# Norms whose reciprocal rms is applied after the product: X turned unscaled, last products by channel half, first products by channel tile

## The chip, the cores and the metric

The kernel runs on one core of one Trainium2 chip. The metric is the device time of one execution in microseconds (us), the median of several. Engines are named as in the profile: PE is TensorE (matmuls; PEld its weight loads), DVE is VectorE, ACT is ScalarE, POOL is GpSimd, SP is SyncE, which only issues loads here. Each engine works through its own instructions strictly in order; semaphores join the engines.

## The reference

The input X (256 tokens x 1024 channels, fp32) goes through nine stages that each add to it: feed-forward, attention with a state-space model, feed-forward (first layer, with modulation by a condition vector c), feed-forward, a mixer of pooling and long convolution ("mix2"), feed-forward, feed-forward, a latent attention ("mix3"), feed-forward, and a last norm. The change is about the norms ahead of the last six stages, which have a gain but no shift:

```python
def rmsnorm(x, g):
    x32 = x.astype(jnp.float32)
    y = x32 * lax.rsqrt(jnp.mean(x32 * x32, axis=-1, keepdims=True) + RMS_EPS)
    return (y * g.astype(jnp.float32)).astype(x.dtype)

def swiglu_2(h, w_gate, w_up, w_down):
    return (jax.nn.silu(h @ w_gate) * (h @ w_up)) @ w_down

# per layer: x = x + 0.5 * swiglu_2(rmsnorm(x, g), ...)
#            x = x + mixer(rmsnorm(x, g), ...)
#            x = x + 0.5 * swiglu_2(rmsnorm(x, g), ...)
# at the end: rmsnorm(x, final_norm_g)
```

The reciprocal rms r is one number per token, so (r x) W = r (x W): it may be applied to the product. In a feed-forward stage only the gate product must have it before the silu; the factor of the up product can be applied to the stage's result. The three norms of the first layer are followed by h (1 + scale) + shift, and keep their form.

## The kernel before

**Stages.** `STAGES` (line 41) lists nine stages, numbered 0 to 8 here: ffn0, mix1, ffn1, ffn2, mix2, ffn3, ffn4, mix3, ffn5. The norm ahead of stage n is norm n; "boundary n" is the stretch from the last product of stage n-1 to the first product of stage n. Norms 3 to 8 have no shift. Norm 9 is the last norm.

**Weights.** All weights pass as panels of 128 x 1024 fp32 (512 KB) through a ring of six slots (`RING`). SP loads a panel into `raw`; ACT makes its fp32r high part `w_hi` (`split_hi`, L177); DVE makes the rest `w_lo` (`split_lo`, L183). Activations are split in the same way, and each product is three matmuls, high x high, high x low, low x high (`product3`, L199). A feed-forward stage has 66 panels: gate, up and down panels for each of 22 tiles of the hidden dimension. Around each boundary the order of panels on DVE is by hand: at the end of each stage DVE and ACT split the first three panels of the next, the fourth comes behind the norm.

**A feed-forward tile f.** PE: gate product, up product (24 matmuls of 256 columns each, into the two halves of one PSUM bank), then the down product of tile f-1 (`token_product`, 12 matmuls of 512 columns into banks 0 to 3, one bank for each of four quarters: two token halves m by two channel halves). After both products ACT takes the silu of the gate (L378), DVE multiplies it by the up product (L411), ACT makes the high part (L381), DVE the low part (L416). DVE's order is: three `split_lo`, then this `hidden(f)`.

**A boundary without shift.** When a quarter of the last product is complete DVE adds it to X (L486, four instructions, in the order of banks). ACT squares and sums each quarter of X (L255), POOL computes r for each token half (`rstd_pool`, L282 and L283), DVE makes a diagonal matrix `diag` of it (L293), PE turns and scales X in one go as a matmul of X with `diag` (L317, 16 fp32 products of 128 x 128, each in two records), ACT writes the high part times the gain (L275), DVE the low part (L303), and the first product of the next stage starts when its first channel tile is there: all eight channel tiles of the gate panel, then all eight of the up panel. The results of stages 0 to 2 are normed and gated before they are added (L493, L500), and norms 0 to 2 have a shift, with two DVE instructions for a channel tile (L306, L308).

**mix2** starts with a product by tokens (panels M2 to M2+3, result copied by ACT at L1595), then has twelve "parts": a channel product, a copy by ACT with a scale (`centre`, L1573), two taps of a short convolution by DVE (L1631, L1634), with one `split_lo` between. A spectrum product (`multiply`, L1645 to L1648) stands between parts 8 and 9, and 10 and 11, on DVE. **mix3** starts with four channel products and a second norm of the latents (`rms_col`, L1901; POOL's power, L1064).

**The end.** Norm 9's r scales X and the row `final_row` (L2124); the row is loaded by POOL behind its last r (L2051); POOL issues the two halves of the output (L2054).

## Time and profile before

| | us |
|---|---|
| median of 3 runs | 1715.95 (1714.08 to 1716.29) |
| span of the profiled execution | 1713.4 |
| PE busy | 1581.6 |
| DVE busy | 1058.8 |
| ACT busy | 716.8 |
| POOL busy | 263.5 |
| mean granted TensorE clock | 0.959 of full speed |

The span runs from the first to the last instruction; the timed runs lie up to 3 us above it. Matmuls are pipelined: a matmul of 256 columns is shown as 0.28 us, but its successor starts 0.12 us after it; for 512 columns these are 0.39 and 0.23 us. So starts, not durations, tell how long PE takes. The granted clock is given as a share of 2.4 GHz: 0.5 is 1.2 GHz.

### The profile page before, as it was taken

To read this page: it belongs to the slowest core of one execution; us is meant where nothing else is said; L and a number is where in the kernel's file an instruction comes from. 1 tells how busy PE (TensorE), PEld (TensorE's weight loads), DVE (VectorE), ACT (ScalarE), POOL (GpSimd) and SP (SyncE) were. 2 spreads that over 40 slices of the span, in tenths; PEclk is the share of its full clock that TensorE was granted. 3 is DMA by queue.
4 is the path that set the end of the run, shared out by engine and by line. 5 is a ranking of instruction groups with operands and counts; after the bars stand their busy time and mean duration, and the time that the engine had idled before them with its cause. 6 is when DMAs were issued, how large, how long until landed. Compare 5 with 4: busy or idle time off the path is not lost.

```text
span 1713.4 us, 28025 instructions
## 1 busy us (share of the span) xinstructions
PE 1581.6 (92%) x10288; PEld 1417.2 (83%) x10288; DVE 1058.8 (62%) x1344; ACT 716.8 (42%) x1145; POOL 263.5 (15%) x264
## 2 busy tenths in 40 slices
PE   4899869899789999899999999999999988999996
PEld 1599858775569999899988789998999987889995
DVE  7779994699566555555555755555555548655553
ACT  3344322432344444544444444444544436454442
POOL 1489951144310000100000000000000000000000
PEclk9799978898989999999999999999999999999998
DMA  6599755340036665655554335555555532245551
GB/s 219 217 335 335 256 190 197 128 135 25 25 111 216 217 217 183 239 184 184 184 160 148 111 124 183 186 186 174 172 184 184 184 123 99 74 148 184 184 184 50
DMA packets 80195, 292.79 MB, mean 171 GB/s; under 512 B 9019, under 2 KB 9372, under 8 KB 79564
## 3 DMA queue, kind: packets, MB, share of 16 engines
q1 hardware_dynamic: 74432, 270.71, 46.7%
q0 software_dynamic: 4784, 19.09, 3.1%
q10 hardware_dynamic: 924, 2.25, 0.4%
q8 instruction: 36, 0.59, 0.1%
q14 instruction: 19, 0.16, 0.0%
HBM read 288.87 MB, written 3.15 MB: 170 GB/s over the span
## 4 chain that ended last, share of the span: by engine, by line
PE 66%; DVE 3%; ACT 3%; POOL 1%; issue 1%; DMA 0%; DVEq 0%; ACTq 0%; POOLq 0%
PE bank L199 61%; PE bank L317 1%; PE bank L1488 1%; ACT arena L255 1%; DVE w_lo L183 1%; PE bank L1501 1%; ACT w_hi L177 0%; PE bank L1812 0%; PE bank L1790 0%; PE bank L1801 0%; ACT h_hi L275 0%; ACT arena L1884 0%; DVE arena L493 0%; POOL arena L1285 0%; ACT arena L1869 0%
## 5 line engine op out<-in xcount | busy, mean ns | idle before, releaser
L199 PE MATMUL bank<-h_hi,w_hi 128*128 128x256 f32 x2376 | 683.8, 288 | 20.7 <-DVE h_lo L308 7.1
L199 PE MATMUL bank<-h_lo,w_hi 128*128 128x256 f32 x2376 | 677.1, 285 | 0.0
L199 PE MATMUL bank<-h_hi,w_lo 128*128 128x256 f32 x2376 | 676.7, 285 | 0.0
L183 DVE TENSOR_TENSOR w_lo<-raw,w_hi 128x1024 fp32r<-128x1024 f32 x458 | 562.1, 1276 | 98.1 <-ACT w_hi L177 96.8
L199 PEld LDWEIGHTS bank<-h_hi,w_hi 128*128 128x128 f32 x2376 | 460.6, 194 | 35.0 <-DVE h_lo L308 9.3
L177 ACT ACTIVATE w_hi<-raw 128x1024 fp32r<-128x1024 f32 x458 | 453.8, 1049 | 31.9 <-PE bank L199 30.8
L199 PEld LDWEIGHTS bank<-h_lo,w_hi 128*128 128x128 f32 x2376 | 460.9, 194 | 5.7 <-issue 1.0
L199 PEld LDWEIGHTS bank<-h_hi,w_lo 128*128 128x128 f32 x2376 | 460.4, 194 | 0.0
L378 ACT ACTIVATE arena<-bank 128x256 f32<-128x256 f32 x132 | 50.5, 383 | 541.9 <-PE bank L199 541.9
L411 DVE TENSOR_TENSOR arena<-arena,bank 128x256 f32<-128x256 f32 x132 | 55.6, 421 | 343.1 <-ACT arena L378 343.1
L199 PE MATMUL bank<-w_hi,f_hi 128*128 128x512 f32 x528 | 209.2, 396 | 15.2 <-DVE f_lo L416 15.2
L199 PE MATMUL bank<-w_hi,f_lo 128*128 128x512 f32 x528 | 208.8, 396 | 0.0
L199 PE MATMUL bank<-w_lo,f_hi 128*128 128x512 f32 x528 | 207.3, 393 | 0.0
L282 POOL TENSOR_SCALAR stat<-stat 128x1 f32<-128x1 f32 x26 | 9.1, 351 | 1062.7 <-ACT arena L255 1062.3
L199 PEld LDWEIGHTS bank<-w_hi,f_hi 128*128 128x128 f32 x528 | 100.7, 191 | 33.3 <-issue 15.6
L199 PEld LDWEIGHTS bank<-w_lo,f_hi 128*128 128x128 f32 x528 | 100.3, 190 | 22.0
L199 PEld LDWEIGHTS bank<-w_hi,f_lo 128*128 128x128 f32 x528 | 100.8, 191 | 16.2
L381 ACT ACTIVATE f_hi<-arena 128x256 fp32r<-128x256 f32 x132 | 55.2, 418 | 118.7 <-DVE arena L411 118.7
L521 DVE SCALAR_TENSOR_TENSOR arena<-arena,stat 128x1024 f32<-128x1024 f32 x70 | 103.7, 1482 | 1.2
L416 DVE TENSOR_TENSOR f_lo<-arena,f_hi 128x256 fp32r<-128x256 f32 x132 | 64.1, 486 | 52.3 <-ACT f_hi L381 52.3
L317 PE MATMUL bank<-diag,X 128*128 128x128 f32 x288 | 42.4, 317 | 24.8 <-DVE diag L293 24.8
L317 PEld LDWEIGHTS bank<-diag,X 128*128 128x128 f32 x288 | 40.7, 229 | 28.3 <-DVE diag L293 28.3
(285 smaller groups left out, 1315.1 us busy)
## 6 DMA issues: line engine op xcount, KB each, us to landing
raw<-panels SPq DMA_DIRECT2D x458, 512.0 KB, 4.5
arena<-ada SPq DMA_DIRECT2D x56, 512.0 KB, 4.9
arena<-ada POOLq DMA_DIRECT2D x16, 512.0 KB, 3.9
spectrum<-arena POOLq DMA_DIRECT2D x2, 1024.0 KB, 7.2
arena<-rows POOLq DMA_DIRECT2D x4, 512.0 KB, 4.1
arena<-spectrum POOLq DMA_DIRECT2D x1, 2048.0 KB, 13.9
X<-x_in SPq DMA_DIRECT2D x1, 1024.0 KB, 5.3
arena<-decay ACTq DMA_DIRECT2D x2, 512.0 KB, 6.6
```

What stands on the lines that cost most here:

```text
L177: act.activation(w_hi[:, slot, :], raw[:, slot, :], ACT.Copy).then_inc(hi_ready, 1)
L183: dve.tensor_tensor(w_lo[:, slot, :], raw[:, slot, :], w_hi[:, slot, :].bitcast(F32), ALU.subtract).then_inc(lo_ready, 1)
L199: last = pe.matmul(out_ap, a, b, start=start and n == 0, stop=stop and n == 2)
L255: return act.activation(squares[:, q, :], source, ACT.Square, scale=D ** -0.5, accum_out=stat[:, at + q:at + q + 1])
L317: mm = pe.matmul(bank[4 + k // 2][:, at:at + P], X[:, m, k * P:(k + 1) * P], diag[:, m, :], start=True, stop=True)
L378: act.activation(ffn_buf[:, f % 2, :], up_bank(f)[:, 0:SEQ], ACT.Silu).then_inc(silu_done, 1)
L381: act.activation(f_hi[:, f % 2, :], ffn_buf[:, 2 + f % 2, :], ACT.Copy).then_inc(f_hi_done, 1)
L411: dve.tensor_tensor(ffn_buf[:, 2 + f % 2, :], ffn_buf[:, f % 2, :], up_bank(f)[:, SEQ:2 * SEQ], ALU.mult).then_inc(hidden_done, 1)
L416: dve.tensor_tensor(f_lo[:, f % 2, :], ffn_buf[:, 2 + f % 2, :], f_hi[:, f % 2, :].bitcast(F32), ALU.subtract).then_inc(f_lo_done, 1)
L521: dve.scalar_tensor_tensor(out=dst, in0=src, scalar=c, in1=dst, op0=ALU.mult, op1=ALU.add).then_inc(ada_used, 1)
L1488: mm = pe.matmul(bank[first_bank + 2 * f + s][:, :], forward[:, s, m, f * P:(f + 1) * P], z_tok[:, m, :], start=m == 0, stop=m == MT - 1)
L1501: mm = pe.matmul(bank[BACK_BANKS[c]][:, 0:SEQ], product[:, 2 * f + s, c * P:(c + 1) * P], inverse[:, s, f, :], start=f + s == 0, stop=f + ...
```

## The change

- **Norms 3 to 8.** X is transposed as it stands, each channel tile when its quarters of X are added, with no wait for r. The turned banks are laid out by channel half. r comes later: ACT squares two quarters ahead of the copies of the high parts and two behind them; POOL and DVE make `diag` behind the eighth low part; behind the first product PE multiplies a matrix of ones with `diag` (`row_pe`), ACT copies the result to `rstd_row` (r along the free axis, the same in all partitions).
- **Where r is applied.** In a feed-forward stage DVE multiplies each gate product by `rstd_row` into `gate_buf`, ACT takes the silu from there, and the result is added to X with r/2. The DVE waits for the gate panel alone, then for the silu, then for the up panel. The up product has a bank of its own. In mix2 ACT's copy of the first product has the scale r, and DVE multiplies each of the twelve parts by `rstd_row` (`scale_part`) ahead of the split of the next panel. In mix3 the latents' mean squares are multiplied by r squared and their diagonals by r, and one more multiplication goes into the keys' rotation.
- **The last two products** of stages 3 to 8 are done by quarters: three quarters of the last but one, two of the last, the fourth of the last but one, the third of the last; the last quarter comes behind the first eight transposes. In front of norms 4 to 8 the order of quarters is channel half 0 of both token halves, then channel half 1.
- **The first product** of every stage is done by channel tile: for a feed-forward stage gate and up of tile k in turn; for mix3 two latent products. This holds for norms 0 to 2 too (mix1 has one panel there).
- **The load** of the last norm's row goes from behind r of norm 9 to behind r of norm 8.

The diff, cut to its core:

```diff
+        def last_two_products(pe, g0, x0, x1, ready, order):
+
+            a, b, c, d = order
+            pe.wait_ge(lo_ready, g0 + 1)
+            for q in (a, b, c):
+                token_quarter(pe, g0, q, *x0, False, False)
+            pe.wait_ge(*ready)
+            pe.wait_ge(lo_ready, g0 + 2)
+            for q in (a, b):
+                token_quarter(pe, g0 + 1, q, *x1, False, True).then_inc(result_ready, 1)
+            token_quarter(pe, g0, d, *x0, False, False).then_inc(panel_used, 1)
+            token_quarter(pe, g0 + 1, c, *x1, False, True).then_inc(result_ready, 1)
+
+        def last_quarter(pe, at):
+
+            kind, n = STAGES[at]
+            x = (f_hi[:, 1, :], f_lo[:, 1, :]) if kind == "ffn" else (h_hi[:, 7, :], h_lo[:, 7, :])
+            token_quarter(pe, FIRST[(kind, n)] + SIZE[kind] - 1, by_quarter(at)[3], *x, False,
+                          True).then_inc(panel_used, 1)
...
+        PLAIN = 3
+
+        def plain(n):
+
+            return PLAIN <= n < len(STAGES)
+
+        def by_quarter(at):
+
+            return (0, 2, 1, 3) if plain(at + 1) and at >= PLAIN else (0, 1, 2, 3)
...
+        def turned_out(n, k):
+
+            b, half = (4 + k % 4, k // 4) if plain(n) else (4 + k // 2, k % 2)
+            return bank[b][:, half * SEQ:(half + 1) * SEQ]
+
+        def of_channel(n, k):
+
+            return KT * n + (k if plain(n) else k | 1) + 1
...
+        def norm_act(act, n):
+
+            if plain(n):
+                norm_act_squares(act, n, 0, 2)
+                norm_act_rest(act, n)
+                norm_act_squares(act, n, 2, 4)
+            else:
+                norm_act_squares(act, n)
+                if n < len(STAGES):
+                    norm_act_rest(act, n)
+
+        def row_act(act, n):
+
+            act.wait_ge(row_product, rows_before(n) + 1)
+            act.activation(rstd_row[:, :], row_bank(n)[:, 0:SEQ], ACT.Copy).then_inc(row_done, 1)
+
+        def row_bank(n):
+
+            return bank[3 if STAGES[n][0] == "ffn" else 6]
+
+        def row_pe(pe, n):
+
+            pe.wait_ge(diag_done, 2 * n + 2)
+            for m in range(MT):
+                mm = pe.matmul(row_bank(n)[:, m * P:(m + 1) * P], ones[:, :], diag[:, m, :], start=True,
+                               stop=True)
+            mm.then_inc(row_product, 1)
...
+        def turn_pe(pe, n, k, m):
+
+            tr = pe.transpose(turned_out(n, k)[:, m * P:(m + 1) * P], X[:, m, k * P:(k + 1) * P], ident[:, :])
+            if m == MT - 1:
+                tr.then_inc(turned, 1)
+
+        def norm_pe(pe, n, first):
+
+            if plain(n):
+                for m in range(MT):
+                    pe.wait_ge(x_done, added(n, 0, m))
+                    for k in range(4):
+                        turn_pe(pe, n, k, m)
+                if n - 1 >= PLAIN:
+                    last_quarter(pe, n - 1)
+                for k in range(4):
+                    pe.wait_ge(h_lo_done, KT * n + k + 1)
+                    first(k)
+                    for m in range(MT):
+                        pe.wait_ge(x_done, added(n, 1, m))
+                        turn_pe(pe, n, 4 + k, m)
+                for k in range(4, KT):
+                    pe.wait_ge(h_lo_done, KT * n + k + 1)
+                    first(k)
+                row_pe(pe, n)
+                return
...
+            def first_up(k):
+
+                if k == 0:
+                    pe.wait_ge(lo_ready, base + 2)
+                    if s0:
+                        pe.wait_ge(hidden_done, s0)
+                w = slice(k * P, (k + 1) * P)
+                for g, out in ((base, gate_out(at, 0)), (base + 1, up_out(at, 0))):
+                    mm = product3(pe, out, w_hi[:, g % RING, w], w_lo[:, g % RING, w], h_hi[:, k, :],
+                                  h_lo[:, k, :], k == 0, k == KT - 1)
+                    if k == KT - 1:
+                        mm.then_inc(panel_used, 1)
...
+                if plain(at):
+                    act.wait_ge(gate_scaled, gates_before(n) + f + 1 + 2 * i)
+                    act.activation(ffn_buf[:, f % 2, :], gate_buf[:, f % 2, :],
+                                   ACT.Silu).then_inc(silu_done, 1)
+                else:
+                    act.wait_ge(panel_used, base + (3 * f + 1 if f else 2) + RING * i)
+                    act.activation(ffn_buf[:, f % 2, :], gate_out(at, f), ACT.Silu).then_inc(silu_done, 1)
...
+                if plain(at):
+                    if f == 0:
+                        dve.wait_ge(row_done, rows_before(at) + 1)
+                    dve.wait_ge(panel_used, base + (3 * f if f else 2) + RING * i)
+                    if s0 + f >= 2:
+                        dve.wait_ge(silu_done, s0 + f - 1 + 2 * i)
+                    dve.tensor_tensor(gate_buf[:, f % 2, :], gate_out(at, f), rstd_row[:, :],
+                                      ALU.mult).then_inc(gate_scaled, 1)
                 dve.wait_ge(silu_done, s0 + f + 1 + 2 * i)
                 if s0 + f >= 2:
                     dve.wait_ge(f_lo_done, s0 + f - 1 + 2 * i)
-                dve.tensor_tensor(ffn_buf[:, 2 + f % 2, :], ffn_buf[:, f % 2, :],
-                                  up_bank(f)[:, SEQ:2 * SEQ], ALU.mult).then_inc(hidden_done, 1)
+                dve.wait_ge(panel_used, base + (3 * f + 1 if f else 2) + RING * i)
+                dve.tensor_tensor(ffn_buf[:, 2 + f % 2, :], ffn_buf[:, f % 2, :], up_out(at, f),
+                                  ALU.mult).then_inc(hidden_done, 1)
...
+        def add_plain_dve(dve, kind, n, at, i):
+
+            q = by_quarter(at)[i]
+            m, x = q // 2, X[:, q // 2, quarter(q)]
+            wait_result(dve, at, kind, n, q)
+            dve.scalar_tensor_tensor(out=x, in0=bank[q][:, :],
+                                     scalar=stat[:, HALF_RS + m:HALF_RS + m + 1] if kind == "ffn" else 1.0,
+                                     in1=x, op0=ALU.mult, op1=ALU.add).then_inc(x_done, 1)
+
+        def boundary_dve(dve, kind, n, at, order):
+
+            if at < PLAIN:
+                add_dve(dve, kind, n, at)
+                if not plain(at + 1):
+                    diag_dve(dve, at + 1)
+                low_dve(dve, at + 1, order)
+                if plain(at + 1):
+                    diag_dve(dve, at + 1)
+                    half_dve(dve, order)
+                return
+            for i in range(3):
+                add_plain_dve(dve, kind, n, at, i)
+            if plain(at + 1):
+                low_dve(dve, at + 1, order, 0, 1)
+                add_plain_dve(dve, kind, n, at, 3)
+                low_dve(dve, at + 1, order, 1, KT)
+                diag_dve(dve, at + 1)
+                half_dve(dve, order)
+            else:
+                add_plain_dve(dve, kind, n, at, 3)
...
+            def first_tokens(k):
+
+                g, w = M2 + k // 2, slice(512 * (k % 2), 512 * (k % 2) + 512)
                 pe.wait_ge(lo_ready, g + 1)
-                for half in range(2):
-                    k, w = 2 * j + half, slice(512 * half, 512 * half + 512)
-                    pe.wait_ge(h_lo_done, KT * 4 + k + 1)
-                    for m in range(MT):
-                        t = slice(m * P, (m + 1) * P)
-                        mm = product3(pe, bank[m][:, :], w_hi[:, g % RING, w], w_lo[:, g % RING, w],
-                                      h_hi[:, k, t], h_lo[:, k, t], k == 0, k == KT - 1,
-                                      weights_move=True)
-                mm.then_inc(panel_used, 1)
+                for m in range(MT):
+                    t = slice(m * P, (m + 1) * P)
+                    mm = product3(pe, bank[m][:, :], w_hi[:, g % RING, w], w_lo[:, g % RING, w],
+                                  h_hi[:, k, t], h_lo[:, k, t], k == 0, k == KT - 1, weights_move=True)
+                if k % 2:
+                    mm.then_inc(panel_used, 1)
+
+            norm_pe(pe, 4, first_tokens)
...
+            row_act(act, 4)
             act.wait_ge(panel_used, M2 + 4)
             for m in range(MT):
-                act.activation(a_tok[:, m, :], bank[m][:, :], ACT.Copy).then_inc(a_evac, 1)
+                act.wait_ge(rstd_done, 2 * 4 + m + 1)
+                act.activation(a_tok[:, m, :], bank[m][:, :], ACT.Copy,
+                               scale=stat[:, RS + m:RS + m + 1]).then_inc(a_evac, 1)
...
+            def scale_part(j):
+
+                dve.wait_ge(panel_used, M2 + 5 + j)
+                dve.tensor_tensor(part[:, j % 2, :], bank[4 + j % 2][:, 0:SEQ], rstd_row[:, :],
+                                  ALU.mult).then_inc(part_scaled, 1)
+
             def taps_of(j):
 
                 dve.wait_ge(conv_centre, j + 1)
                 tile = (j + 8) % 12
-                src, dst = bank[4 + j % 2], conv[:, j, :]
+                src, dst = part[:, j % 2, :], conv[:, j, :]
...
             dve_panels(dve, M2 + 3, 4)
+            dve.wait_ge(row_done, rows_before(4) + 1)
             for j in range(8):
+                scale_part(j)
                 split_lo(dve, M2 + 7 + j)
                 taps_of(j)
             dve.wait_ge(m2_loaded, 16 * 5)
             for f in range(2):
                 multiply(0, 0, f)
                 for j in (8 + 2 * f, 9 + 2 * f):
+                    scale_part(j)
...
+            order(dve.tensor_tensor(rstd_squared, stat[:, RS:RS + 2], stat[:, RS:RS + 2], ALU.mult))
             dve.wait_ge(latent_sums, 1)
             for j, width in ((0, 256), (2, 128)):
-                dve.tensor_scalar(rms_col[:, j:j + 2], bank[3][:, j:j + 2], 1.0 / width, EPS, ALU.mult,
+                order(dve.tensor_tensor(rms_col[:, j:j + 2], bank[3][:, j:j + 2], rstd_squared, ALU.mult))
+                dve.tensor_scalar(rms_col[:, j:j + 2], rms_col[:, j:j + 2], 1.0 / width, EPS, ALU.mult,
                                   ALU.add).then_inc(rms_mean, 1)
-            diagonals_dve(dve, 4, (rms_pow, 2), latent_diag)
+            dve.wait_ge(rms_pow, 2)
+            for j in range(4):
+                dve.tensor_scalar(rms_diag[:, j, :], ident[:, :], rms_col[:, j:j + 1],
+                                  stat[:, RS + j % 2:RS + j % 2 + 1], ALU.mult,
+                                  ALU.mult).then_inc(latent_diag, 1)
...
+            order(dve.tensor_tensor(k_turn[r, 0, :], k_turn[r, 0, :], k_turn[r, 1, :], ALU.add))
+            dve.wait_ge(row_done, rows_before(7) + 1)
+            dve.tensor_tensor(k_turn[r, 0, :], k_turn[r, 0, :], rstd_row[r, :],
+                              ALU.mult).then_inc(k_rope_done, 1)
...
-                if at + 1 == len(stages):
+                if at == 7:
                     pool.dma_start(final_row, rows[6:7, :].partition_broadcast(P)).then_inc(final_loaded, 16)
```

## Rows read from the trace of the kernel before

**Rows 1.** The page: busy time, share of the span and instructions of PE.
```profile
PE 1581.6 (92%) x10288; PEld 1417.2 (83%) x10288; DVE 1058.8 (62%) x1344; ACT 716.8 (42%) x1145; POOL 263.5 (15%) x264
```
**Rows 2.** Waits of PE: line, releaser, total us, times, longest.
```profile
PE bank L317 <- DVE diag L293: 24.8, 9, 5.4
```
**Rows 3.** Timeline, PE, boundary 6: start us, us, instructions [idle before, releaser].
```profile
1190.36 0.40 PE L199 MATMUL bank<-w_hi,f_hi 128*128 128x512 f32 x1
...
1195.60 0.39 PE L199 MATMUL bank<-w_lo,f_hi 128*128 128x512 f32 x1
1197.54 3.84 PE L317 MATMUL bank<-diag,X 128*128 128x128 f32 x32 [1.55 <-DVE diag L293]
1201.58 0.35 PE L199 MATMUL bank<-h_hi,w_hi 128*128 128x256 f32 x1 [0.20 <-DVE h_lo L303]
```
**Rows 4.** The same timeline, DVE.
```profile
1192.83 1.22 DVE L183 TENSOR_TENSOR w_lo<-raw,w_hi 128x1024 fp32r<-128x1024 f32 x1 [0.53 <-ACT w_hi L177]
1193.99 2.73 DVE L486 SCALAR_TENSOR_TENSOR X<-bank,X 128x512 f32<-128x512 f32 x4
...
1198.55 0.29 DVE L293 TENSOR_SCALAR diag<-ident,stat 128x128 f32<-128x128 f32 x1 [1.07 <-POOL stat L283]
1200.94 3.23 DVE L303 SCALAR_TENSOR_TENSOR h_lo<-bank,C,h_hi 128x256 fp32r<-128x256 f32 x8 [2.11 <-ACT h_hi L275]
```
**Rows 5.** The same timeline, ACT.
```profile
1190.56 0.38 ACT L378 ACTIVATE arena<-bank 128x256 f32<-128x256 f32 x1 [4.37 <-PE bank L199]
...
1196.75 0.63 ACT L255 ACTIVATE arena<-X 128x512 f32<-128x512 f32 x1
...
1200.07 3.03 ACT L275 ACTIVATE h_hi<-bank,C 128x256 fp32r<-128x256 f32 x8 [2.60 <-PE bank L317]
...
1207.77 0.38 ACT L378 ACTIVATE arena<-bank 128x256 f32<-128x256 f32 x1 [2.78 <-PE bank L199]
```
**Rows 6.** Timeline, PE, in mix2: eight plain transposes of 128 x 128.
```profile
928.94 1.03 PE L1511 MATMUL bank<-ident,arena 128*128 128x128 f32 x8
```
**Rows 7.** Busy us (instructions) of PE, PEld, DVE, ACT, POOL by stretch; PEclk, DMA, GB/s.
```profile
200.00:240.00 40.00, 23.17 (x122) 20.67 (x123) 39.96 (x17) 7.33 (x11) 37.86 (x15) 0.72 0.45 157
...
700.00:702.00 2.00, 2.00 (x12) 2.00 (x11) 0.00 (x0) 0.00 (x0) 2.00 (x4) 0.50 0.70 178
...
1190.36:1201.58 11.22, 9.47 (x59) 8.01 (x57) 5.94 (x11) 6.02 (x16) 1.71 (x4) 1.00 0.27 99
...
1480.00:1482.00 2.00, 1.90 (x11) 1.79 (x10) 1.69 (x4) 1.41 (x4) 0.00 (x0) 0.63 0.00 0
```
**Rows 8.** Timeline, DVE, mix2 from the first spectrum product to the last tap.
```profile
943.57 1.23 DVE L183 TENSOR_TENSOR w_lo<-raw,w_hi 128x1024 fp32r<-128x1024 f32 x1
...
960.28 0.48 DVE L1634 SCALAR_TENSOR_TENSOR arena<-bank,C,arena 128x255 f32<-128x255 f32 x1
```
**Rows 9.** Timeline, boundary 3, DVE and PE.
```profile
694.43 2.74 DVE L500 SCALAR_TENSOR_TENSOR X<-arena,stat,X 128x512 f32<-128x512 f32 x4
...
698.35 5.69 PE L317 MATMUL bank<-diag,X 128*128 128x128 f32 x32 [5.41 <-DVE diag L293]
```
**Rows 10.** Timeline, boundary 2: ACT's first silu, and DVE's last low part.
```profile
510.04 0.38 ACT L378 ACTIVATE arena<-bank 128x256 f32<-128x256 f32 x1 [5.12 <-PE bank L199]
...
506.02 0.42 DVE L308 TENSOR_TENSOR h_lo<-arena,h_hi 128x256 fp32r<-128x256 f32 x1
```
**Rows 11.** Timeline, DVE, ffn0: behind its first product, and in its middle.
```profile
89.35 0.42 DVE L411 TENSOR_TENSOR arena<-arena,bank 128x256 f32<-128x256 f32 x1 [3.65 <-ACT arena L378]
...
215.37 14.66 DVE L183 TENSOR_TENSOR w_lo<-raw,w_hi 128x1024 fp32r<-128x1024 f32 x3
```
**Rows 12.** The page's groups: busy us, mean ns | idle of the engine before.
```profile
L411 DVE TENSOR_TENSOR arena<-arena,bank 128x256 f32<-128x256 f32 x132 | 55.6, 421 | 343.1 <-ACT arena L378 343.1
```
**Rows 13.** Timeline, the end: r of norm 9, and the last scaling.
```profile
1699.66 0.56 POOL L283 TENSOR_TENSOR stat<-stat 128x1 f32<-128x1 f32 x1
...
1704.04 2.48 DVE L2124 SCALAR_TENSOR_TENSOR arena<-X,stat,arena 128x1024 f32<-128x1024 f32 x2 [5.61 <-DMA arena<-rows]
```

212 lines of the change are left out of this document (126 added, 86 removed).

## The prediction

> **What bounds the kernel now.** The page first: PE is busy for 1581.6 of 1713.4 us [rows 1], so in most places only less PE work could help, and the change removes nearly none. The waits of PE come next: 24.8 us in 9 pieces, one for each norm, for the diagonal matrix of r [rows 2]. So I read the boundaries. In boundary 6 PE starts the last but one product at 1190.36, issues the last matmul of stage 5 at 1195.60, idles 1.55 us, turns X for 3.84 us and starts stage 6 at 1201.58 [rows 3]. The wait is a relay: DVE adds four quarters from 1193.99 [rows 4], ACT's last square starts at 1196.75 [rows 5], POOL then makes r, DVE the diagonal at 1198.55 [rows 4]; ACT's first high part waits for the turned X until 1200.07 [rows 5], DVE's low part until 1200.94 [rows 4]. Boundaries 4, 5, 7 and 8 repeat this to 0.1 us. Inside a feed-forward tile DVE waits 343.1/132 = 2.6 us for the silu [rows 12]: there PE is the bound, with room on DVE. Last, the end: the final scaling waits 5.61 us, and what ends the wait is a load [rows 13].
>
> **Boundary 6, worked out.** Time t runs from 1190.36, the start of the last but one product. A silu starts 0.20 us after the matmul behind its product (1190.56 against 1190.36), so the second up/gate pair of stage 6 starts at 1207.77 - 0.20, t = 17.2 [rows 3, 5]. This is what the change must bring forward. A quarter of a product is 3 matmuls of (1195.60 - 1190.36)/23 = 0.228 us, so 0.68; a tile of the first pair is 6 matmuls of 0.12, so 0.72 us.
> - The new order has the quarters of the first channel half out at 2.73 and 3.41, the third at 4.78 (each shows 0.2 later). DVE is held by one `w_lo` before its adds. That ends now at t = 3.7 [rows 4]; as the multiplication no longer stands behind the silu (0.4), at 3.3. Adds at 0.68 (a quarter of 2.73 [rows 4]): 3.3 to 4.7, the third 5.0 to 5.7.
> - A plain transpose takes (1.03 - 0.27)/7 = 0.11 us [rows 6], a product with the diagonal 3.84/16 = 0.24 [rows 3]. The first eight: 4.8 to 5.65; then the last quarter to 6.3. ACT's two squares end at 5.4, its first high part (0.49) at 5.95, the low part at 6.5. So the first product starts at 6.5 instead of 11.2: 4.7 us won.
> - Given back: eight more transposes (0.9) and the fourth add, out at 7.2, for which PE waits some 0.4. The eight tiles end at about 13.6. Then the row of r: squares 3 and 4 stand on ACT behind the eighth high part (about 11.1), end at 12.5; POOL takes twice 0.95 (the 0.56 of its power [rows 13] and an addition before it, with gaps), the second r out at 14.0, DVE 0.3: 14.4 with its handovers. PE waits 0.8 for it, issues 0.5, and goes on at 14.9. Here the wait for r comes back, shortened, behind the first product.
> - Sum: 17.2 - 14.9 = **2.3 us**. Lower bound 1.0 (each handover 0.1 worse), upper 3.7 (no wait for the row).
> Behind it DVE splits two panels by 17.0, and PE needs the first at 17.8, the second at 20.7; the first hidden tile is ready by 19.4 and needed at 20.7. The cover is thin but there.
> Boundaries 5, 6 and 8: 3 x 2.3 = **6.9**. Boundary 7 too, but mix3's chain of the latents' rms gets two small ordered instructions (0.2 each, as nothing hides them): **1.9**.
>
> **Boundary 4 and mix2.** The first product of mix2 has 12 matmuls of 512 columns for two tiles, 1.37 us a tile. Tiles 6 and 7 need the fourth panel's `w_lo`, which DVE does behind `diag`, and ACT's `w_hi` behind squares 3 and 4. With a tile each 1.37 us (plus transposes) the eighth high part ends only at 13.4, the squares at 14.8, `diag` at 16.5, `w_lo` at 17.9; PE wanted it at 15.5. So 2.4 us of waiting; the product and its row end at 21.4 instead of 22.2: 0.8 won. Then DVE's stretch from 943.57 to 960.28 + 0.48 = 960.76 [rows 8], where it works nearly through and PE waits for it at both ends: four more multiplications, 4 x 0.42, as an instruction of this size takes [rows 12], and the split at 943.57, which now stands behind the scaling of part 8 and so behind PE. Worked through, the last tap ends 0.8 us later on an unchanged start: 1.6 us lost on the shifted one. Together **-0.8** (-2.5 to +1). The other eight multiplications fall in 2.9 us periods of which 2.7 are then filled: hidden.
>
> **Boundary 3.** The gated adds stay. Now `diag` waits for all of them [rows 9]; then the turned quarters follow the adds of 694.43 to 697.17 directly, ACT copies at 697.0 (two squares first), the first product starts at 698.1 instead of 704.24 (698.35 + 5.69 + 0.20). PE's clock matters here: it idled for 5.41 us and its 16 products took 5.69 us instead of 3.84 [rows 3, 9], at 1.2 GHz until after 702 [rows 7]. I let the slow stretch last until 701.8 also after the change, which costs 1.85 us of the first product. Row of r by 707.0, next pair at 707.5 instead of 710.2: **2.7** (1.5 to 4.6, the latter at full clock).
>
> **Boundaries 2 and 0.** Two DVE instructions a tile pace the first product, and the up product then stands behind. With both products by tile the up product fits: DVE ends at 506.44 [rows 10], PE 0.75 later, at 507.2, instead of 509.84 (510.04 - 0.20): **2.6** (1.5 to 2.9). In ffn0 the same brings 2.6 to 4.5 at first, since PE's clock was low there, and DVE idled 3.65 us behind it [rows 11]. But in the middle of ffn0 DVE is the bound: from 200 to 240 us it is busy 39.96, with POOL at 37.86, PE at 23.17 [rows 7], and three splits take 14.66 us instead of 3.5 [rows 11]. POOL's work doesn't move. What DVE did ahead survives in my reading: **2.5** (0 to 4.5). Boundary 1 has one panel by tile, as before: 0.
>
> **Tiles of ffn2 to ffn5.** 88 multiplications of 0.42 us, and a wait for the silu inside DVE's sequence. Per tile DVE then needs 3.5 for splits, 0.5 waiting for `w_hi`, 0.42 scaling, 0.46 for the silu, 1.32 from the multiplication to the low part: 6.2 of the 8.5 us that PE takes (24 x 2 x 0.12 + 12 x 0.228). PE's row product and the transposes are in the sums above. Cost at nothing; the cover is 2.3 us a tile.
>
> **The end.** Without the load the first scaling can follow the last add, and the second one the second r, out at 1699.66 + 0.56 = 1700.22; with 1.28 us for it (the two take 2.48) it ends at 1701.5 instead of 1706.52 [rows 13]. **5.0** (4.5 to 5.6). The load moves to the start of ffn5 on POOL's queue, where POOL has nothing else; panels there are six ahead.
>
> **Sum.** 6.9 + 1.9 - 0.8 + 2.7 + 2.6 + 2.5 + 5.0 = 20.8 us on the profiled span of 1713.4: 1692.6. The median lies 2.55 above that span: 1715.95 - 20.8 = **1695**. The forecast's own range: 1687 to 1703.
>
> **Rivals.**
> - *The clock falls at the boundaries.* Around 1480, in a stretch of waits and plain transposes, the granted clock was 0.63 [rows 7]; in boundary 6, with idle time and the diagonal products, it stayed at 1.00 [rows 7]. The new boundary has transposes in place of such products. If each of the five boundaries 4 to 8 loses to it what boundary 3 lost (5.69 - 3.84 = 1.85 us [rows 3, 9]), 9.2 is given back: 1704. Against it: the quiet stretch is now 0.9 us of transposes with no idle, less than half the one near 1480. The Trainium skill, "TensorE: Matmul & The Clock Gate", Part 4 on the PE-mode transpose, says that transposes don't count as busy for the clock as matmuls do; the rows near 1480 agree with it, but had idle time too. By that rule boundary 3, too, would keep its slow stretch. Chance 12%.
> - *The relay doesn't shorten.* PE's in-order queue has waits for single adds and single low parts; if a handover I took as done in time is late (the third add, the low part behind it), the first product starts early and stops again, and the row of r ends where the diagonal did. Then boundaries 3 to 8 bring nothing, and 0 and 2 and the end bring 10.1: 1706. Against it: the bare transposes need no r. Chance 8%.
> - *Slower: DVE becomes the bound of the tiles.* Place: hidden(f) of ffn2 to ffn5. The gain of 20.8 and a loss over 3.4 need 24.2/88 = 0.28 us a tile, so a DVE sequence of 8.8 us against my 6.2, 2.6 more than worked out; it decides from 8.5 on. At 8.8 the time is about 1719. For it: DVE now waits three times inside a tile, before only twice; against: its idle time of 2.6 us a tile [rows 12] is more than the 0.9 added. Chance 4%.
> - *The change brings more*: full clock in boundary 3, all of 4.5 kept in ffn0, no wait for the row: 1686. Chance 8%.
>
> **How the numbers follow.** Forecast 68% at 1695; clock 12% at 1704, no relay 8% at 1706, more 8% at 1686, slower 4% at 1719. The range 1686 to 1706 holds all but the slower case and tails. 0.2% is 3.4 us, about what a measurement of this kernel can tell from no change: faster than 1712.5 has 93%, within 1712.5 to 1719.4 3%, slower 4%.
>
> **What would show it.** In boundary 6: no diagonal product; first product of the stage 6.5 us after the last but one product of the stage before begins; a wait of PE of about 0.8 us for `diag` behind the eighth tile. In boundary 4: a wait of some 2.4 us for `w_lo`. In mix2: DVE's last tap later against the first spectrum product. In ffn2 to ffn5: 8.5 us from silu to silu, unchanged. At the end: no wait for a load. Granted clock 1.00 over boundaries 4 to 8. Wrong if silus stand further apart than 8.5 us, if the clock shows 0.5 behind the transposes, or if ffn0 ends no earlier.

## The result, and the profile after

| | before | after |
|---|---|---|
| median | 1715.93 us | 1692.85 us (1686.63 to 1694.82, four runs) |
| ratio after/before | | 0.9867, interval 0.9847 to 0.9887 |
| span of the profiled execution | 1713.4 us | 1692.1 us |
| PE busy | 1581.6 us | 1572.3 us |
| PE waits for `diag` | 24.8 us in 9 | 11.7 us in 3, and 3.5 us in 5 for the row |

Predicted were 1695 us for the median and 1692.6 for the span. The page and the waits of PE, after (what waited, on what, total us, times, longest):

```profile
PE 1572.3 (93%) x10216; PEld 1405.0 (83%) x10216; DVE 1102.4 (65%) x1454; ACT 728.2 (43%) x1151; POOL 263.5 (16%) x264
...
PE bank L424 <- DVE diag L368: 11.7, 3, 5.4
...
PE bank L199 <- DVE w_lo L183: 9.0, 3, 4.5
...
PE bank L356 <- DVE diag L368: 3.5, 5, 0.8
```

The 24.8 us of [rows 2] are now 11.7 (norms 0 to 2, which still have the diagonal product, L424) and 3.5 (the row of r, L356). Boundary 6 in PE's timeline after, and two rows each of ACT and DVE; it answers to [rows 3 to 5]:

```profile
1179.78 0.40 PE L199 MATMUL bank<-w_hi,f_hi 128*128 128x512 f32 x1
...
1184.57 1.03 PE L397 MATMUL bank<-ident,X 128*128 128x128 f32 x8
...
1186.36 0.39 PE L199 MATMUL bank<-h_hi,w_hi 128*128 128x256 f32 x1
...
1190.22 0.38 PE L397 MATMUL bank<-ident,X 128*128 128x128 f32 x2
...
1194.27 0.71 PE L356 MATMUL bank<-diag,ones 128*128 128x128 f32 x4 [0.79 <-DVE diag L368]
...
1191.62 0.62 ACT L294 ACTIVATE arena<-X 128x512 f32<-128x512 f32 x1
...
1193.93 0.28 DVE L368 TENSOR_SCALAR diag<-ident,stat 128x128 f32<-128x128 f32 x1 [0.84 <-POOL stat L330]
```

With t counted from 1179.78 the first eight transposes start at 4.79 (worked out: 4.8), the first product at 6.58 (6.5), the last square at 11.84, the second diagonal at 14.15, the row product at 14.49 after a wait of 0.79 (0.8). PE goes on at 14.96 (14.9); the next pair started at 17.2 before. The end, after ([rows 13]): the second scaling starts 0.04 us after the second r is out (1683.65 + 0.56), and no load stands ahead of it.

```profile
1682.13 1.27 DVE L2357 SCALAR_TENSOR_TENSOR arena<-X,stat,arena 128x1024 f32<-128x1024 f32 x1
...
1683.65 0.56 POOL L330 TENSOR_TENSOR stat<-stat 128x1 f32<-128x1 f32 x1
...
1684.25 1.28 DVE L2357 SCALAR_TENSOR_TENSOR arena<-X,stat,arena 128x1024 f32<-128x1024 f32 x1 [0.84 <-POOL stat L330]
```

To see where the time went, one takes the same instruction in both traces (a silu, an add, the first product behind a stage's second pair) and follows the difference of its two times. What a stretch adds to this difference is what it won in this one execution:

| stretch | predicted | measured |
|---|---|---|
| up to norm 0 | 0 | 0.4 |
| boundary 0 and the rest of ffn0, boundary 1, mix1 | 2.5 | 4.4 + 1.3 - 1.1 = 4.6 |
| boundary 2 | 2.6 | 2.5 |
| boundary 3 | 2.7 | 3.0 |
| boundary 4 and mix2 | +0.8 - 1.6 = -0.8 | -0.9 - 1.3 = -2.2 |
| boundaries 5, 6, 8 | 3 x 2.3 = 6.9 | 3 x 2.2 = 6.6 |
| boundary 7 and mix3 | 1.9 | 1.3 |
| tiles of ffn2 to ffn5 | 0 | 0.0 |
| end | 5.0 | 5.0 |
| sum | 20.8 | 21.3 |

The measured rows are rounded, so they add up to 21.2. Two of them vary between executions by more than they miss by: what lies ahead of ffn1, and boundary 7 with mix3 (first and last experiment).

### The profile page after: what moved, and what is told of

The parts are those of the page before. It is cut to its first block, busy times and chain, and to the rows that moved or that the text cites. A ratio compares the mean times of both kernels' runs of the same rounds, so it can differ in the third digit from the quotient of the medians.

```text
span 1692.1 us, 28192 instructions
## 1 busy us (share of the span) xinstructions
PE 1572.3 (93%) x10216; PEld 1405.0 (83%) x10216; DVE 1102.4 (65%) x1454; ACT 728.2 (43%) x1151; POOL 263.5 (16%) x264
## 4 chain that ended last, share of the span: by engine, by line
PE 67%; DVE 3%; ACT 2%; POOL 1%; issue 1%; ACTq 0%; DVEq 0%; POOLq 0%
PE bank L199 62%; PE bank L1686 1%; PE bank L1699 1%; PE bank L2015 1%; ACT arena L294 1%; PE bank L397 1%; PE bank L2037 1%; DVE w_lo L183 0%; PE bank L2026 0%; POOL stat L330 0%; DVE arena L646 0%; POOL stat L329 0%; ACT arena L2112 0%; POOL arena L1481 0%; ACT arena L2097 0%
## 5 line engine op out<-in xcount | busy, mean ns | idle before, releaser
L524 ACT ACTIVATE arena<-arena 128x256 f32<-128x256 f32 x88 | 36.8, 418 | 195.2 <-DVE arena L565 195.2
L706 DVE SCALAR_TENSOR_TENSOR arena<-arena,stat 128x1024 f32<-128x1024 f32 x70 | 107.9, 1541 | 1.2
L528 ACT ACTIVATE arena<-bank 128x256 f32<-128x256 f32 x44 | 16.8, 382 | 167.0 <-PE bank L199 167.0
L1481 POOL TENSOR_TENSOR arena<-arena 128x512 f32<-128x512 f32 x32 | 46.4, 1471 | 53.6 <-DVE arena L1514 53.6
```

Source lines behind the costliest of these rows:

```text
L524: act.activation(ffn_buf[:, f % 2, :], gate_buf[:, f % 2, :], ACT.Silu).then_inc(silu_done, 1)
L706: dve.scalar_tensor_tensor(out=dst, in0=src, scalar=c, in1=dst, op0=ALU.mult, op1=ALU.add).then_inc(ada_used, 1)
L1481: pool.tensor_tensor(rot_out[:, s % 2, 2 * part:2 * part + 2, :], z, r, ALU.mult).then_inc(rot_done, 1)
```

## The experiments

Executions of one kernel lie up to 11 us apart, so an effect of a few us is read from the traces, stretch by stretch, and the medians only say that nothing contradicts. Where a stretch from norm to norm is given, it runs from one "first eight transposes" row to the next; after has them at 880.18, 993.81, 1184.57, 1375.37 and 1489.84 (norms 4 to 8), so 113.63, 190.76, 190.80 and 114.47 us.

**The changed kernel again**, unedited, on the chip of the next three.

> The changed kernel once more, as the base for the other runs of this chip. All theories expect about 1693 us, a ratio of 0.987 to the kernel before; its single runs so far lay between 1686.6 and 1694.8. In boundary 6 a wait of PE of 0.8 us for the diagonal, in boundary 4 one of 2.4 us for the fourth panel, with the granted clock at 0.5 behind it.

Measured: 1691.16 us, ratio 0.986 (0.9843 to 0.9876). Norm 4 to 5 takes 113.62 us and 5 to 6 takes 190.74: this part repeats to 0.02. What differs between executions lies elsewhere. Up to norm 2 all eleven traces of the changed kernel and of its variants below run the same instructions, yet norm 2's diagonal product starts between 483.46 and 492.64 us in them (488.51 in after, 485.98 in after_again, 493.61 before). Counted as in the table's second row, from norm 0 to norm 2, the win is 4.7 us in after, 7.0 in after_again, and 3.6 to 9.4 in all. Mix3 is the other such place (last experiment).

**The load alone.** The kernel before, with

```diff
-                if at + 1 == len(stages):
+                if at == 7:
                     pool.dma_start(final_row
```

> The kernel before with the load of the last norm's row alone moved behind r of norm 8. The forecast's term is 5.0 us: 1715.9 - 5.0 = 1710.9, ratio 0.9971, and the last scaling ends about 1.3 us behind the second r. Rival: the load at the start of the last stage delays panels there; then the last stage is longer than before and the gain under 4 us.

Measured: 1709.24 us, 5.5 under before's 1714.70 on this chip, ratio 0.9965 (0.9953 to 0.9977). In its trace the second scaling waits for r and no longer for a DMA:

```profile
1699.56 1.40 POOL L283 TENSOR_TENSOR stat<-stat 128x1 f32<-128x1 f32 x1
...
1700.99 1.28 DVE L2124 SCALAR_TENSOR_TENSOR arena<-X,stat,arena 128x1024 f32<-128x1024 f32 x1 [0.45 <-POOL stat L283]
```

The profiled execution is 4.5 us shorter (1708.9 against 1713.4); POOL's last instruction for r took 1.40 us there instead of the 0.56 of before and after, which is not explained. So the term stands by itself at 4.5 to 5.5, a fifth to a fourth of the gain, for one moved line. The last stage is no longer than before: its first down product starts at 1521.96 us against 1522.07, the additions to X at 1695.59 against 1695.69.

**The first pair by channel tile, alone.** The kernel before, in ffn0 and ffn1 with

```diff
-            up(0)
+            if n < 2:
+                ...
+                for k in range(KT):
+                    ...
+                    for g, out in ((base, bank[0][:, 0:SEQ]), (base + 1, bank[2][:, 0:SEQ])):
+                        mm = product3(pe, out, ..., k == 0, k == KT - 1)
+            else:
+                up(0)
```

> The kernel before with the first pair of products of ffn0 and ffn1 done by channel tile (gate and up in turn, the up product in a bank of its own), nothing else. Theory: boundary 2 gains 2.5 us, boundary 0 some 4.4 us, as PE stays busy enough there for a granted clock of 1.00; together 5.5 to 7, time 1709 to 1710.5. Rival, the sum of the prediction: 2.6 + 2.5 = 5.1 with part of the gain of boundary 0 lost where DVE and POOL bound ffn0. Second rival: the clock there differs between executions whatever the order is, and only 2.6 + 2.6 comes.

Measured: 1707.91 us, ratio 0.9959 (0.9947 to 0.9971), 6.8 us less; the sum had 2.6 + 2.5 = 5.1, which the interval (5.0 to 9.1 us) just allows, so the traces must tell. The first silu of ffn0 starts at 83.59 instead of 88.94, and 0.9 of these 5.35 us were won ahead of the first channel tile, so the pair's order brought 4.4. Boundary 2 brought 2.5: the lead over before grows from 7.86 at norm 2's diagonal product (485.75) to 10.38 at the first down product (505.22). First the kernel with only the load moved (its ffn0 is that of before), at 80 to 82 and 84 to 88 us, then this one, then after, at 84 to 88 (columns: PE, PEld, DVE, ACT, POOL busy with counts, granted clock, DMA share, GB/s):

```profile
80.00:82.00 2.00, 1.70 (x7) 1.21 (x8) 1.93 (x5) 1.98 (x2) 0.00 (x0) 0.75 0.00 0
...
84.00:88.00 4.00, 4.00 (x21) 4.00 (x21) 1.83 (x2) 0.00 (x0) 3.94 (x2) 0.52 0.52 145
```
```profile
84.00:88.00 4.00, 4.00 (x36) 4.00 (x35) 2.99 (x5) 2.84 (x4) 3.65 (x4) 1.00 0.72 227
```
```profile
84.00:88.00 4.00, 4.00 (x36) 4.00 (x35) 2.99 (x5) 2.76 (x5) 3.65 (x3) 1.00 0.55 162
```

With one product PE did three matmuls for each channel tile of DVE; the tiles came 0.92 us apart and PE waited 0.30 us for each, and the clock fell near 81 us, inside this product; the up product behind it then ran slowly (84 to 88 us: 0.52). It did so in both traces with one product. With two products interleaved the clock stayed at 1.00 from 80 us to the first silu in all twelve traces, and the order brought 4.4 us in each of them. The pace alone is not the cause, though: in boundary 2 of the same two traces the same single product, with the same waits, ran at 1.00 throughout, and there the order brings 2.5. What makes the difference between the two boundaries was not tested. The 1.9 us between 4.4 and 2.5 is what my 2.5 left at the upper end of its range. They are not lost in the middle of ffn0 either, where DVE and POOL are full: by the end of ffn0 the lead was never smaller than at the first silu (0.6 to 2.4 us larger in the twelve traces).

**Ordinary products in place of transposes.** The changed kernel, X turned by

```diff
-            tr = pe.transpose(..., X[:, m, k * P:(k + 1) * P], ident[:, :])
+            tr = pe.matmul(..., X[:, m, k * P:(k + 1) * P], ident[:, :], start=True, stop=True)
```

> The changed kernel with X turned by an ordinary fp32 product with the identity instead of PE's transpose: 0.24 us instead of 0.10 for each of 16. Theory: the first product of a stage starts 8 x 0.14 = 1.1 us later, each of its first four tiles takes 0.28 more, all of this on the path (the wait for the row of r follows the eighth tile and stays): 2.2 us for each of boundaries 4 to 8 and less for boundary 3, 11 to 12 us in all, about 1704. Rival (the clock): if transposes let the clock fall, ordinary products would hold it up, and the loss would be smaller, in boundary 4 above all.

Measured: 1701.01 us (1694.46 to 1705.13), ratio 0.9906 (0.9886 to 0.9927), 9.9 more than the changed kernel on this chip. The profiled execution had lost 4.1 us to after's before norm 3, where the two kernels are the same; from norm 3 to ffn5 it loses 7.2, less than the 9.9 of the medians and the 11 to 12 expected (1.6 in boundary 6, for 2.2 expected). So the plain transpose is worth a third of the gain by the trace: the first eight take 1.95 us in 16 passes,

```profile
1191.21 1.95 PE L397 MATMUL bank<-ident,X 128*128 128x128 f32 x16
...
1202.51 0.71 PE L356 MATMUL bank<-diag,ones 128*128 128x128 f32 x4 [0.81 <-DVE diag L368]
```

and the row product comes 11.30 us after them instead of 9.70. In boundary 3 it is the other way round. Granted clock there (third to last column), first of after, whose first transposes start at 687.66, then of this kernel, where they start at 691.79:

```profile
690.00:692.00 2.00, 1.60 (x7) 0.61 0.03 8
692.00:694.00 2.00, 2.00 (x12) 0.54 0.00 0
694.00:696.00 2.00, 2.00 (x19) 1.00 0.00 0
```
```profile
692.00:694.00 2.00, 1.83 (x15) 1.00 0.00 0
694.00:696.00 2.00, 1.58 (x14) 1.00 0.05 8
696.00:698.00 2.00, 2.00 (x20) 1.00 0.00 0
```

Both waited 2.29 us for the gated adds. Behind the wait come transposes, or products with the same operands; from four to six us after the first transposes the granted clock was 0.50 in nine traces of ten and 0.57 in the tenth (in one of the nine, extra_8, it had fallen before they began); with products, in the one trace there is, it never left 1.00. The row of r came at 10.96 us behind the first turn instead of 11.43, though PE had twice the passes. The Trainium skill, "TensorE: Matmul & The Clock Gate", Part 4, says that transposes don't count as busy for the clock in the way matmuls do; boundary 3 agrees with it, on one trace with products. One trace is not enough to show it: behind the wait in boundary 4 the clock stayed up in one execution of eight with no change there, and in this very kernel it fell there, from the third matmul behind the wait of 2.37 us on, though X was turned by products.

**The fourth panel earlier.** The changed kernel; DVE and ACT split mix2's fourth panel between channel tiles 4 and 5 of norm 4:

```diff
             for k in range(KT):
+                if n == 4 and k == 4:
+                    split_hi(act, M2 + 3)
                 act.wait_ge(turned, of_channel(n, k))
...
-            act_panels(act, M2 + 3, 4)
+            act_panels(act, M2 + 4, 3)
```

and the same for DVE with `split_lo` and `dve_panels`.

> The changed kernel with mix2's fourth panel split between the fourth and the fifth channel tile of norm 4, on ACT and DVE, instead of behind the diagonal. Theory: PE's wait of 2.36 us in boundary 4 goes, and with it the fall of the granted clock behind it (six matmuls of 512 columns at 0.43 instead of 0.23 us, and the row's product): mix2 starts its parts 4.0 us earlier, -4.0 us in the time, granted clock 1.00 through the boundary. Rival: the clock falls there for another reason (the transposes); then the wait alone goes, -2.4 us, and some window behind the turn still shows less than 1.00.

Measured: 1690.52 us, ratio 0.9866 (0.9845 to 0.9886); median against median only 0.6 less than the changed kernel, which ran on another chip, and by the ratios (0.9866 against 0.986) nothing. In the trace norm 4 to norm 5 takes 109.39 us instead of 113.63: 4.24 less, where 4.0 were expected. What the medians don't show of it lies in the spread of other stretches: this execution came into norm 4 1.15 us later than the one of after, and its five runs lie between 1686.67 and 1695.05. Here is the spot, PE after:

```profile
891.03 0.39 PE L199 MATMUL bank<-w_lo,h_hi 128*128 128x512 f32 x1
893.78 0.47 PE L199 MATMUL bank<-w_hi,h_hi 128*128 128x512 f32 x1 [2.36 <-DVE w_lo L183]
...
895.24 0.63 PE L199 MATMUL bank<-w_hi,h_hi 128*128 128x512 f32 x1
895.67 0.63 PE L199 MATMUL bank<-w_hi,h_lo 128*128 128x512 f32 x1
...
897.80 1.01 PE L356 MATMUL bank<-diag,ones 128*128 128x128 f32 x4
898.51 0.42 PE L199 MATMUL bank<-h_hi,w_hi 128*128 128x256 f32 x1
```

and in the kernel with the row moved (next experiment), which has this boundary unchanged:

```profile
891.66 0.39 PE L199 MATMUL bank<-w_lo,h_hi 128*128 128x512 f32 x1
894.41 0.47 PE L199 MATMUL bank<-w_hi,h_hi 128*128 128x512 f32 x1 [2.37 <-DVE w_lo L183]
...
895.86 0.39 PE L199 MATMUL bank<-w_hi,h_hi 128*128 128x512 f32 x1
896.08 0.39 PE L199 MATMUL bank<-w_hi,h_lo 128*128 128x512 f32 x1
...
897.22 0.61 PE L356 MATMUL bank<-diag,ones 128*128 128x128 f32 x4
897.59 0.36 PE L199 MATMUL bank<-h_hi,w_hi 128*128 128x256 f32 x1
```

The same wait; in the first the six matmuls from 895.24 stand 0.43 us apart, at the clock's lower level (896 to 898 us: granted 0.50), in the second 0.23. From the last matmul ahead of the wait to the first of the parts it is 7.48 us against 5.93: the fall costs 1.55 us. It was there in seven of the eight traces with this wait (1.83 us in one of them), and in none of the three without it.

**The row of r later.** The changed kernel, in stages 3, 5, 6 and 8 with the row's product behind the second gate product, in mix3 behind the third latent product (norm 4 keeps its place):

```diff
                 channel_product(pe, gate_out(at, f), g, i)
+                if f == 1 and plain(at):
+                    row_pe(pe, at)
                 channel_product(pe, up_out(at, f), g + 1, i)
```

> The changed kernel with the product that spreads r into a row issued behind the next product (the second gate tile, in mix3 the third latent product) instead of ahead of it. Theory: PE's wait for the diagonal (0.79 us in boundaries 5, 6 and 8, about the same in 7, 0.28 in 3) is covered: -3.3 us in all. Rival: the row then comes late for the first hidden tile, whose low part was ready with 1.3 us to spare; if the spare time is gone PE waits for f_lo ahead of the first down product, and nothing or less is won.

Measured: 1689.64 us, ratio 0.9854 (0.9842 to 0.9867). Norm 5 to 6 and 6 to 7 take 189.84 and 189.90 instead of 190.76 and 190.80: 0.9 us a boundary, the 0.79 of the wait and a little more. Norm 3 to 4 takes 192.15 instead of 192.52, 0.4 less, of which 0.28 is its wait. Boundary 8 gains 0.1 only, where PE waits 0.69 us for `f_lo` instead. Now DVE waits for the row:

```profile
1195.35 0.42 DVE L568 TENSOR_TENSOR arena<-bank,arena 128x256 f32<-128x256 f32 x1 [0.56 <-ACT arena L346]
```

So the move brings 2.3 us of the 3.3 expected. (Norm 4 to 5 is 1.64 shorter too, by luck: the clock didn't fall there, see above.) Norm 7 to 8 was 0.5 longer (114.97). I took that for the price of the row moved in mix3, wrongly (last experiment).

**Both moves.**

> Both moves. Theory: they are in different places, so -4.0 - 3.3 = -7.3 us against the changed kernel, about 1684 where that has 1691. Rival: as for each alone, -2.4 or less.

Measured: 1686.78 us (1680.03 to 1688.38), ratio 0.9837 (0.982 to 0.9855). Norm 4 to 5 takes 109.41 us, 5 to 6 takes 189.84 and 6 to 7 189.90: the two effects add, 6.0 us with 0.6 more in boundary 3, and lie apart. The version is faster than the kernel before; that it is faster than the changed kernel is shown by these stretches, while the intervals of the two ratios (this one, and 0.9843 to 0.9876) overlap.

**The channel half order undone.** The changed kernel with the quarters of the last products always in bank order:

```diff
-            return (0, 2, 1, 3) if plain(at + 1) and at >= PLAIN else (0, 1, 2, 3)
+            return (0, 1, 2, 3)
```

> The changed kernel with the quarters of the last two products and the adds in the order of banks 0, 1, 2, 3 in front of norms 4 to 8 too. Theory: the first turn of the second token half must then wait for the third add instead of the second, so the last quarter and the first product start later, 0.7 to 1.0 us for each of five boundaries: +3.5 to +5 us. Rival: the wait for the row of r ends at the same time whatever the order is, and takes it up: under +1 us.

Measured: 1693.62 us, ratio 0.9885 (0.987 to 0.99): 2.5 more than the changed kernel by the medians of two chips, but the trace doesn't show 3.5 to 5. PE in boundary 6, where the stage's last product but one starts at 1180.03:

```profile
1184.82 0.60 PE L397 MATMUL bank<-ident,X 128*128 128x128 f32 x4
1185.83 0.66 PE L397 MATMUL bank<-ident,X 128*128 128x128 f32 x4 [0.41 <-DVE X L663]
...
1194.64 0.71 PE L356 MATMUL bank<-diag,ones 128*128 128x128 f32 x4 [0.29 <-DVE diag L368]
```

The wait of 0.41 us that the order avoids is there; but the wait for the row sinks from 0.79 to 0.29, and the row product starts at t = 14.61 instead of 14.49. So 0.1 us a boundary is what the order brings. My expectation counted the first wait and forgot that the second, behind it in PE's queue, ends at a time of its own. What else the 2.5 of the medians holds stays open.

**DVE's cover in the tiles.** The changed kernel with eight more DVE instructions in each tile of ffn2 to ffn5, and then with twelve:

```diff
                     dve.tensor_tensor(gate_buf[:, f % 2, :], ...).then_inc(gate_scaled, 1)
+                    for e in range(8):
+                        dve.tensor_tensor(spare_rows[:, e, :], rstd_row[:, :], rstd_row[:, :], ALU.mult)
```

> Eight more DVE products of 128x256 behind the scaling of the gate, in each of the 88 tiles of ffn2 to ffn5; they write rows that nobody reads. In the trace of after, where DVE lags behind PE, a tile takes it 6.17 us (one gate scaling at 1202.78, the next at 1208.95), and one product of this size is followed 0.34 us later by the next where nothing lies between. Theory 1 (the tiles have a cover of 2.3 us, and the added work fills DVE's wait of 0.48 us for the silu first): 6.17 + 8 x 0.34 - 0.48 = 8.41 us a tile, under PE's 8.5: 0 to 5 us in all, the tiles behind a boundary included. Theory 2 (the same cover, but the added products are spaced like dependent ones, 0.46 us): 9.4 us a tile, +75 us. Rival (DVE is already the bound of the tiles): +2.7 x 88 = 240 us.

> The same with twelve products a tile. Theory 1: 6.17 + 12 x 0.34 - 0.48 = 9.77 us a tile against PE's 8.5, so 1.27 us a tile come out: 88 x 1.27 = 110 us (95 to 125). Theory 2: 11.2 us a tile, +240 us. Rival (DVE already the bound): +4.1 x 88 = 360 us. If the cover of 2.3 us a tile is right, the time of extra_8 and of this one differ by about 100 us although both add work of the same kind in steps of four.

Measured: 1710.1 us with eight, 18 more than the changed kernel; 1829.23 with twelve (ratio 1.0674), 137 more. First DVE after, two tiles where it catches up behind boundary 6, then a tile of the kernel with eight:

```profile
1202.78 0.42 DVE L565 TENSOR_TENSOR arena<-bank,arena 128x256 f32<-128x256 f32 x1
...
1208.95 0.42 DVE L565 TENSOR_TENSOR arena<-bank,arena 128x256 f32<-128x256 f32 x1
```
```profile
1248.64 0.42 DVE L566 TENSOR_TENSOR arena<-bank,arena 128x256 f32<-128x256 f32 x1
1248.97 2.76 DVE L569 TENSOR_TENSOR arena<-arena 128x256 f32<-128x256 f32 x8
1251.65 0.42 DVE L574 TENSOR_TENSOR arena<-arena,bank 128x256 f32<-128x256 f32 x1
...
1257.00 0.42 DVE L566 TENSOR_TENSOR arena<-bank,arena 128x256 f32<-128x256 f32 x1
```

DVE's sequence is 6.17 us in the changed kernel and 8.36 with eight more (expected 8.41), the wait for the silu filled. PE then waits 0.26 us once at the start of a stage and in no tile behind it, but again at the end of stages 3, 5 and 6, for the low part of the last hidden tiles:

```profile
1192.25 0.50 PE L199 MATMUL bank<-w_hi,f_hi 128*128 128x512 f32 x1 [2.74 <-DVE f_lo L579]
```

Norm 5 to norm 6 is 3.6 us longer (194.33), norm 3 to 4 is 4.6, norm 6 to 7 is 3.0 and ffn5 0.7: 11.9 of the 16.5 us by which the profiled execution is longer than after's. The rest lies where the two kernels hardly differ. I had expected 0 to 5, because I looked at the tiles and not at their end. From eight to twelve it is 119 us, 4 x 0.34 x 88 = 120. Theory 1 holds for the tiles, and DVE as their bound is out: that would have cost 240 and 360.

**Mix2's multiplications.** The changed kernel, `scale_part` twice for parts 8 to 11:

```diff
                 dve.wait_ge(panel_used, M2 + 5 + j)
+                if j >= 8:
+                    dve.tensor_tensor(diag..., bank[4 + j % 2][:, 0:SEQ], rstd_row[:, :], ALU.mult)
                 dve.tensor_tensor(part[:, j % 2, :], ...).then_inc(part_scaled, 1)
```

> In mix2 the multiplication by r of parts 8 to 11 is done twice (the second result goes to a place that nobody reads): four more DVE products of 128x256. Theory (DVE's stretch behind the first spectrum products is what sets the end there, so the change's four multiplications cost what four instructions take): 4 x 0.34 to 4 x 0.42, the stretch from the turned tiles of norm 4 to those of norm 5 grows by 1.4 to 1.7 us over after's 113.63. Rival (PE or ACT sets the end of that stretch, and the 1.3 us lost in mix2 have another cause): it grows by less than 0.3 us. The time of the whole kernel moves by too little to tell; the trace decides.

Measured: 1695.55 us, which tells nothing; norm 4 to norm 5 takes 114.60 us instead of 113.63, 0.97 more: neither 1.4 to 1.7 nor under 0.3. DVE's rows of the second to fourth added instruction (the first stands at 940.41, behind a wait of 3.76), and of the first gate behind them:

```profile
943.29 0.42 DVE L1834 TENSOR_TENSOR diag<-bank,arena 128x256 f32<-128x256 f32 x1
943.63 0.41 DVE L1835 TENSOR_TENSOR arena<-bank,arena 128x256 f32<-128x256 f32 x1
...
950.40 0.42 DVE L1834 TENSOR_TENSOR diag<-bank,arena 128x256 f32<-128x256 f32 x1
...
953.24 0.42 DVE L1834 TENSOR_TENSOR diag<-bank,arena 128x256 f32<-128x256 f32 x1
...
956.08 0.48 DVE L1867 SCALAR_TENSOR_TENSOR arena<-bank,stat,arena 128x256 f32<-128x256 f32 x1
```

The four cost 0.97, as three at 0.34 each would (an instruction's distance to the next, not its 0.42). The first fills a wait: after, the scaling of part 9 waits 0.41 us for PE, and here part 9's pair doesn't wait. So DVE bounds the stretch, as the prediction had it, at 1.0 us for four instructions. The change's own loss in mix2 was 1.3; no run takes its four multiplications out.

**Both moves without norm 7.** As both moves, but with the row of norm 7 where the change has it.

> Both moves (the fourth panel of mix2 split between channel tiles 4 and 5 of norm 4; the product of the row of r behind the second gate product), but for norm 7, whose row product stands where the change has it. With the row moved in norm 7 too, the stretch between the turned tiles of norms 6 and 8 shrank by 0.40 us only, of which boundary 6 is worth 0.9: so 0.5 us were lost in mix3. Theory: the stretch from norm 6 to norm 8 shrinks by 0.9 us against after's 305.27, and norm 4 to norm 5 by 4.2, norm 5 to norm 6 by 0.9: about 6.5 us under the changed kernel in the traces, around 1685 us. Rival (the 0.5 has another place): norm 6 to norm 8 as with all rows moved, 304.87.

Measured: 1687.03 us (1686.17 to 1689.13), ratio 0.9848 (0.9831 to 0.9864). Norm 4 to 5, 5 to 6 and 6 to 7: 109.38, 189.86, 189.90, as expected. Norm 6 to 8 takes 303.11 us, against 302.84 with all rows moved and 305.27 after. So neither theory was right, and the 0.5 is no price that can be put on the row of norm 7: norm 7 to 8 (boundary 7 and mix3) takes 112.9, 113.2, 113.4, 114.3, 114.5, 115.0 and 116.6 us in seven kernels that hardly differ there, and the granted clock differs. The stretch from 50 to 60 us behind norm 7's first transposes, in after and with both moves (PE alone):

```profile
1425.37:1435.37 10.00, 9.69 (x50) 0.71 0.16 52
```
```profile
1413.19:1423.19 10.00, 9.83 (x71) 1.00 0.15 52
```

PE is as busy in both, at 50 matmuls in one and 71 in the other. Why the clock differs there was not tested.

## Why the prediction was right

- *Boundaries 5, 6 and 8.* The relay worked out held to 0.1 us at each of its steps until the diagonal. PE goes on at 14.96 where 14.9 was worked out, and 2.2 us each were won instead of 2.3. Mechanism and size stand. The rival without a shortened relay is out. How the 2.2 divide among the unscaled turn, the last products by quarters and the first product by channel tile rests on this reading of the relay: no run has one of the three alone in stages 3 to 8.
- *Boundary 4.* The wait of 2.4 us for the fourth panel was foreseen and was 2.36. What failed is the sign of its term: +0.8 became -0.9, because the clock fell behind that wait, which cost 1.55 (without it, about +0.65). The prediction's own list has "granted clock 1.00 over boundaries 4 to 8" as what would show it, so here it was wrong. It had a rival for the clock, with transposes as its cause at all of the boundaries 4 to 8; it fell at one of them, behind idle time, and where only transposes and a wait of 0.8 us lay it stayed at 1.00.
- *Mix2.* 1.6 predicted, 1.3 measured. The added multiplications of the experiment cost 0.34 each and not 0.42, and one of four fell into a wait; that this is also where the change's own 0.3 went is likely, not shown.
- *Boundary 3.* 2.7 predicted, 3.0 measured, and its parts fit. All its times come 7.6 us earlier, as that much was won ahead of it: the first product at 690.39 (worked out 698.1 - 7.6 = 690.5), the end of the slow clock near 693.8 (701.8 - 7.6 = 694.2), the row of r at 699.09 (699.4), the next pair at 699.56 (699.9).
- *Boundaries 2 and 0.* 2.6 for boundary 2 was right. In ffn0 the term was too small: 4.4 us by the first silu, near the upper bound of 4.5, since with the two products interleaved the clock also stayed at 1.00. The rest of its 4.6, as far as mix1, is spread: 3.6 to 9.4 in eleven executions, all above the predicted 2.5. The worry that the middle of ffn0 eats it was wrong.
- *Boundary 7.* 1.9 predicted, 1.3 measured, inside the 3.7 us by which this stretch varies between kernels that hardly differ there.
- *Tiles.* 6.2 us worked out, 6.17 measured; the cover of 2.3 us a tile is real, but not for the last tiles of a stage.
- *The end.* 5.0 predicted and measured; alone it brought 5.5 by the medians and 4.5 in its trace. The measured 5.0 is 4.7 up to the last scaling, as r came 0.3 later behind the last matmul, and 0.3 behind it, where nothing was predicted.

The misses nearly cancel: ffn0 gave 2.1 more, the start 0.4 and boundary 3 0.3; boundary 4 with mix2 gave 1.4 less, boundaries 5 to 8 0.9. The sum was closer than its terms, and that it met the span to 0.5 us is luck: four executions of the changed kernel lie between 1686.63 and 1694.82, and the median came out 2 us under the forecast.

## What to carry to other kernels

When a wait is moved or removed, follow the next wait in the same queue: it ends at a time of its own, and takes back what was won ahead of it (the channel half order, 0.4 won and 0.3 given back; the row of r). Price an instruction on a full engine by its distance to the next one, 0.34 us here, not by its own 0.42. A short wait of PE can cost more than itself through the clock (here 2.4 us of waiting and, in seven executions of eight, some 1.55 of slow matmuls), so a panel that comes 2.4 us late is worth splitting earlier: this move and the later row made a version of 1686.8 us. And before a difference of a few us is explained, look how far the same stretch spreads in kernels that are the same there.
